# Layer-norm sums of a decoder step: chunks added elementwise on GpSimd before one product with ones on TensorE

## The reference

```python
def layer_norm(x, g, b):
    xf = x.astype(jnp.float32)
    mu = jnp.mean(xf, -1, keepdims=True)
    var = jnp.mean(jnp.square(xf - mu), -1, keepdims=True)
    y = (xf - mu) * lax.rsqrt(var + LN_EPS) * g.astype(jnp.float32) + b.astype(jnp.float32)
    return y.astype(x.dtype)
...
    def post_norm(x, delta, i, j):
        return layer_norm(ALPHA * x + delta, ln_gain[i, j], ln_bias[i, j])

    def half_ffn(x, i, f, j):
        return post_norm(x, 0.5 * swiglu(x, ffn_w_gate[i, f], ffn_w_up[i, f], ffn_w_down[i, f]), i, j)
...
        xp, xs = half_ffn(xp, i, 0, 0), half_ffn(xs, i, 0, 0)
...
        xp, xs = post_norm(xp, yp, i, 1), post_norm(xs, ys, i, 1)
        xp, xs = half_ffn(xp, i, 1, 2), half_ffn(xs, i, 1, 2)
```

## Time and profile before

| | |
|---|---|
| time, median of 3 runs | 3068.14 us (3064.81 to 3071.11) |
| the profiled execution | 3065.47 us, of which the span of instructions is 3063.6 us |
| PE busy | 2847.6 us, 93% of the span |
| DVE, ACT, POOL busy | 1034.4, 821.4 and 524.2 us (34%, 27%, 17%) |
| mean granted clock of PE | 0.964 |

### The profile page before, as it was taken

One profiled execution on the slowest core, in us unless ns is written; L12 is line 12 of the kernel. 1 busy time (PEld: TensorE's weight loads), 2 busy tenths in 40 slices (PEclk: granted clock), 3 DMA queues, 4 the chain that ended last, 5 costly groups with the idle time before them and its releaser, 6 DMA issues. The chain is left out here.

```text
span 3063.6 us, 56299 instructions
## 1 busy us (share of the span) xinstructions
PE 2847.6 (93%) x23010; PEld 2684.4 (88%) x23010; DVE 1034.4 (34%) x1683; ACT 821.4 (27%) x1590; POOL 524.2 (17%) x581
## 2 busy tenths in 40 slices
PE   8999999868999998999999999999967778899998
PEld 7999989748999998999989899989955447899998
DVE  2222233645222224222243424443442222522223
ACT  2222122623222212222122424242332221322222
POOL 3222102011222201222102021102110001222210
PEclk9999999979999999999999999999979888999999
DMA  7776624013666644666423142314247873466641
GB/s 248 241 246 182 222 67 98 4 50 108 221 220 209 200 133 153 210 219 223 156 67 91 44 125 78 95 40 120 83 149 277 293 275 109 154 220 207 229 143 42
DMA packets 460485, 478.73 MB, mean 156 GB/s; under 512 B 55886, under 2 KB 433951, under 8 KB 456120
## 3 DMA queue, kind: packets, MB, share of 16 engines
q1 hardware_dynamic: 454880, 464.85, 46.3%
q0 software_dynamic: 5392, 11.67, 1.3%
q10 hardware_dynamic: 64, 0.08, 0.0%
HBM read 463.55 MB, written 198.59 MB: 216 GB/s over the span
## 5 line engine op out<-in xcount | busy, mean ns | idle before, releaser
L703 PE MATMUL bank<-sb_xh,sb_wl 128*128 128x272 f32 x4416 | 957.7, 294 | 56.0 <-DVE sb_wl L1439 28.3
L707 PE MATMUL bank<-sb_xh,sb_wh 128*128 128x272 f32 x4416 | 943.5, 290 | 0.0
L705 PE MATMUL bank<-sb_xl,sb_wh 128*128 128x272 f32 x4416 | 941.7, 290 | 0.0
L1439 DVE TENSOR_TENSOR sb_wl<-sb_raw,sb_wh 128x1024 fp32r<-128x1024 f32 (+1 forms) x340 | 454.5, 1337 | 999.0 <-ACT sb_wh L1184 990.9
L703 PEld LDWEIGHTS bank<-sb_xh,sb_wl 128*128 128x128 f32 x4416 | 711.5, 191 | 64.4 <-DVE sb_wl L1439 31.7
L705 PEld LDWEIGHTS bank<-sb_xl,sb_wh 128*128 128x128 f32 x4416 | 712.6, 191 | 0.6
L707 PEld LDWEIGHTS bank<-sb_xh,sb_wh 128*128 128x128 f32 x4416 | 708.6, 191 | 0.0
L1184 ACT CAST sb_wh<-sb_raw 128x1024 fp32r<-128x1024 f32 (+1 forms) x340 | 376.6, 1110 | 980.4 <-PE bank L707 965.2
L703 PE MATMUL bank<-sb_hh,sb_wl 128*128 128x272 f32 x1408 | 312.9, 294 | 0.0
L705 PE MATMUL bank<-sb_hl,sb_wh 128*128 128x272 f32 x1408 | 304.9, 287 | 0.0
L707 PE MATMUL bank<-sb_hh,sb_wh 128*128 128x272 f32 x1408 | 304.7, 287 | 0.0
(11 more groups left out here) (240 smaller groups left out, 2273.3 us busy)
## 6 DMA issues: line engine op xcount, KB each, us to landing
out_state_b_s<-in_cache_b_kv SPq DMA_DIRECT2D x176, 704.0 KB, 6.3
sb_dkvb<-in_cache_b_kv SPq DMA_DIRECT2D x144, 512.0 KB, 6.3
sb_raw<-in_ffn_w_gate SPq DMA_DIRECT2D x88, 512.0 KB, 3.9
sb_raw<-in_ffn_w_up SPq DMA_DIRECT2D x88, 512.0 KB, 4.3
sb_raw<-in_ffn_w_down SPq DMA_DIRECT2D x64, 704.0 KB, 4.7
sb_raw<-in_attn_b_w_qkv SPq DMA_DIRECT2D x72, 512.0 KB, 3.9
out_state_b_s<-in_cache_b_kv SPq DMA_DIRECT2D x32, 1016.0 KB, 7.7
out_state_b_s<-in_cache_b_kv SPq DMA_DIRECT2D x44, 176.0 KB
```

Source lines behind the costliest of these rows:

```text
L703: pe.matmul(acc(s, h), wl[slot][:, k, :], hi(k)[:, halves[h]], start=start and k == 0, stop=False)
L705: pe.matmul(acc(s, h), wh[slot][:, k, :], lo(k)[:, halves[h]], start=False, stop=False)
L707: last = pe.matmul(acc(s, h), wh[slot][:, k, :], hi(k)[:, halves[h]], start=False, stop=end)
L1439: dve.tensor_tensor(wl[j % 2][:, 0:ph.chunks, :], raw[j][:, 0:ph.chunks, :], v.bitcast(F32), ALU.subtract).then_inc(wl_rdy, 1)
```

## The change

The chunks ahead of the last ones (seven of eight in a down phase, six of eight in a wo phase) no longer go through PE one by one. POOL adds them, chunk upon chunk, into `sil[0]`, and their squares into `sil[1]` (`sums` on POOL, behind `centre`), and PE takes one product of ones with each of the two (`sums` on PE, behind `half_done`, four matmuls). The last chunk or two go through `stats` by halves as before and add to the same banks. ACT's `square` now waits on POOL's additions (`q_add`) instead of PE's reads.

```diff
+            def sums(n):
+
+                pe.wait_ge(s_add, add0[n + 1])
+                for h in range(2):
+                    pe.matmul(bank[4 + h][:, 0:HALF], ones[:], sil[0][:, halves[h]], start=True, stop=False)
+                pe.wait_ge(q_add, add0[n + 1])
+                for h in range(2):
+                    mm = pe.matmul(bank[6 + h][:, 0:HALF], ones[:], sil[1][:, halves[h]], start=True, stop=False)
                 mm.then_inc(st_read, 1)
...
                     if i == 2:
                         centre(n)
-                    if i == 5:
-                        stats(n, 0)
-                    if i >= 5 and i % 2:
-                        stats(n, (i - 3) // 2)
                 weights_ready(14)
                 acc_ready(ph, n, 7)
                 part(14, (0,))
-                stats(n, 6)
                 weights_ready(15)
                 part(15, (0,)).then_inc(half_done, 1)
+                sums(n)
                 part(14, (1,), range(3))
-                stats(n, 7, (0,))
+                stats(n, 7, 0)
...
-                    if i >= 4:
-                        stats(n, 2 * i - 8)
-                        stats(n, 2 * i - 7)
                 for i in (6, 7):
                     pe.wait_ge(wl_rdy, ph.u0 + i + 5)
                     acc_ready(ph, n, i)
                     mm = part(i, (0,))
-                    if i == 6:
-                        stats(n, 4)
                 mm.then_inc(half_done, 1)
-                stats(n, 5)
+                sums(n)
                 part(6, (1,), range(3))
...
                 if m >= 2:
-                    act.wait_ge(st_read, sq_count(n, m - 2))
+                    act.wait_ge(q_add, add0[n] + max(m - 2, 1))
...
+            def sums(n):
+
+                pool.wait_ge(z0_rdy, n + 1)
+                for m in range(1, add0[n + 1] - add0[n] + 1):
+                    for h in range(2):
+                        pool.wait_ge(z_add[h], KC * n + m + 1)
+                    if m > 1:
+                        pool.wait_ge(s_add, add0[n] + m - 1)
+                    pool.tensor_tensor(sil[0][:], z[:, 0, :] if m == 1 else sil[0][:], z[:, m, :], ALU.add).then_inc(s_add, 1)
+                    pool.wait_ge(sq_rdy, sq_count(n, m))
+                    if m > 1:
+                        pool.wait_ge(q_add, add0[n] + m - 1)
+                    pool.tensor_tensor(sil[1][:], sqb[0][:] if m == 1 else sil[1][:], sqb[m % 2][:], ALU.add).then_inc(q_add, 1)
```

More of the change, by code:

```diff
@@ L234, in build @@
         c_mm, c_rdy, z_sh, z0_rdy = (sem(n) for n in ("c_mm", "c_rdy", "z_sh", "z0_rdy"))
-        sq_rdy, st_read = sem("sq_rdy"), sem("st_read")
+        sq_rdy, st_read, s_add, q_add = sem("sq_rdy"), sem("st_read"), sem("s_add"), sem("q_add")
         ln_msq, ln_dev, ln_rs, ln_nrm, ln_xh = (sem("ln_" + n) for n in ("msq", "dev", "rs", "nrm", "xh"))
@@ L456, in build @@
         TAIL = {"down": [(7, 0), (7, 1)], "wo": [(6, 0), (7, 0), (6, 1), (7, 1)]}
-        sq_events, sq0 = [], [0]
+        sq_events, sq0, st0, add0 = [], [0], [0], [0]
         for ph in phases:
@@ L462, in build @@
                 sq0.append(sq0[-1] + len(sq_events[-1]))
+                st0.append(st0[-1] + 1 + len(TAIL[ph.kind]))
+                add0.append(add0[-1] + first - 1)
         def sq_count(n, m, h=None):
@@ L466, in sq_count, with st_count @@
             return sq0[n] + (ev.index((m, None)) if (m, None) in ev else ev.index((m, h))) + 1
+        def st_count(n, m, h):
+            ev = sq_events[n]
+            return st0[n] + 2 + ev[add0[n + 1] - add0[n] + 1:].index((m, h))
         FIRST_KS = 3
@@ L568, in load_bias @@
                 if ps is pass_a or ps is pass_b[0]:
-                    sp.wait_ge(st_read, sq0[norm_index(0 if ps is pass_a else 1, 0) + 1])
+                    sp.wait_ge(st_read, st0[norm_index(0 if ps is pass_a else 1, 0) + 1])
                 else:
@@ L754, in centre, with stats @@
                 mm.then_inc(c_mm, 1)
[L756 to L766, removed]
-                mm.then_inc(st_read, 1)
+            def sums(n):
[5 more added lines that the diff above has]
+                    mm = pe.matmul(bank[6 + h][:, 0:HALF], ones[:], sil[1][:, halves[h]], start=True, stop=False)
+                mm.then_inc(st_read, 1)
+            def stats(n, m, h):
+                pe.wait_ge(z_add[h], KC * n + m + 1)
+                pe.matmul(bank[4 + h][:, 0:HALF], ones[:], z[:, m, halves[h]], start=False, stop=m == KC - 1)
+                pe.wait_ge(sq_rdy, sq_count(n, m, h))
+                pe.matmul(bank[6 + h][:, 0:HALF], ones[:], sqb[m % 2][:, halves[h]], start=False, stop=m == KC - 1).then_inc(st_read, 1)
             def acc_ready(ph, n, m):
@@ L807, in project_down @@
                     first_unit(ph.next, n + 1, range(FIRST_KS))
-                stats(n, 7, (1,))
+                stats(n, 7, 1)
             def project_wo(ph, n):
@@ L829, in project_wo @@
                     mm = part(i, (0,))
-                    if i == 6:
-                        stats(n, 4)
                 mm.then_inc(half_done, 1)
-                stats(n, 5)
+                sums(n)
                 part(6, (1,), range(3))
-                stats(n, 6, (0,))
-                stats(n, 7, (0,))
+                stats(n, 6, 0)
+                stats(n, 7, 0)
                 part(6, (1,), range(3, KC)).then_inc(mm_done, 1)
                 part(7, (1,)).then_inc(mm_done, 1)
-                stats(n, 6, (1,))
+                stats(n, 6, 1)
                 first_unit(ph.next, n + 1, range(FIRST_KS))
-                stats(n, 7, (1,))
+                stats(n, 7, 1)
             def tokens_major(R, b):
@@ L1206, in square @@
                 if m >= 2:
-                    act.wait_ge(st_read, sq_count(n, m - 2))
+                    act.wait_ge(q_add, add0[n] + max(m - 2, 1))
                 elif n:
-                    act.wait_ge(st_read, sq0[n])
+                    act.wait_ge(st_read, st0[n])
                 w = slice(0, TOK) if h is None else halves[h]
@@ L1213, in mean_square @@
             def mean_square(n, h):
-                act.wait_ge(st_read, sq_count(n, KC - 1, h))
+                act.wait_ge(st_read, st_count(n, KC - 1, h))
                 act.activation(sqb[0][:, halves[h]], bank[4 + h][:, 0:HALF], ACT.Square).then_inc(ln_msq, 1)
@@ L1928, in _ @@
                     centre(n_norm)
+                    sums(n_norm)
                     n_norm += 1
```

## The result

The changed kernel takes 3012.49 us (median of 4 runs, 3011.98 to 3014.24), the kernel before beside it 3067.77 (3064.81 to 3071.11): ratio 0.9819, 95% interval 0.9804 to 0.9835. That is 55.3 us faster where 61.8 were forecast. The time lies 7.5 us above the point and half a us inside the upper end of the forecast, 2996 to 3013; one of the four runs (3014.24) lies beyond it. The profiled execution took 3012.28 us, and its span is 3010.4 us.

The account below looks back on a forecast made before the run. PE was taken to bound the norm phases; 62.6 us of removed matmuls less 0.4 and 0.4 of waits gave 61.8 us, so 3003.7 or 3006.3, stated as 3005. The forecast range was 2996 to 3013 (0.83); 8 in 10, 2996 to 3020.

Parts of the forecast that it names:

- What is removed: PE's `stats` groups ahead of the half-0 tail: 11.04 us per down phase, 9.20 per wo phase, together 62.6 us.
- The small waits: PE waiting for unit 15's split, 0.1 us per down phase, and for POOL's last additions, 0.2 us per wo phase.
- POOL's additions in a down phase: The two additions for chunk 6, 1.74 us each with gap, end at about 420.7, hidden at no cost.
- the sign of being right: Among the signs listed for a right prediction: POOL's additions take 1.4 to 1.6 us.
- The cover of 4.6 us: End of a down phase: time left between POOL's last addition, about 420.7, and PE's product on `sil[1]`, 425.33.
- The first rival: POOL and DVE hold each other up in every addition, at 2.75 + 0.17 us each: 3025.9 us, chance 0.10.
- POOL in wo: End of a wo phase: POOL's last three additions end at 719.7 against PE's need at 719.51, cost 0.2 us.
- ACT's new wait: Squares wait for POOL's additions with ACT's weight splits queued behind: no cost, 4.2 us of cover at the tightest, in wo.
- the tail: Behind `half_done`, the chain from the last half-0 `stats` to POOL's scaling moves as a whole, keeping about 29 us.
- The slower rival: POOL sets the pace and the kernel is slower: 3083.7 us at 5.5 us per addition and gap, chance 0.03.
- The clock ... is no case of its own: Clock drops in the norm tails, 2.5 us each, may shift by norm; this only widens the forecast.
- The 6 us allowed for the tails: Clock drops in two or three of six norm tails, either way, as a widening of the forecast.

Follow-up runs that it names:

- dve_adds: The changed kernel with all 68 additions on DVE and none on POOL: 2999.83 us, ratio 0.9792 to the kernel before.
- pool_twice: The changed kernel with each of POOL's 68 additions made twice, first into an unused buffer: 3030.11 us, ratio 0.9890 to the kernel before.
- after_again: The changed kernel once more, unchanged, on another chip: 3000.95 us, ratio 0.9809 to the kernel before.

## Why the prediction was right, and where it was off

- **What is removed**, 11.04 us in a down and 9.20 in a wo phase: 10.97 and 9.16 measured (the first down phase 10.15, since its centring began 1.24 us later in the kernel before, and that stretch was 0.8 shorter there than in the other two). The six norms together gained 61.3 us where the sum said 61.8. This is shown, also by dve_adds.
- **The small waits**: 0.1 us was taken for unit 15 in a down phase, and some 0.08 is there, behind DVE's subtraction as the prediction had it; 11.04 less that is the 10.97 measured. For the 0.2 us of a wo phase there is nothing: PE has no idle time ahead of L767 and L770.
- **POOL's additions in a down phase**, 1.74 us with gap: there is no gap, and the additions of squares behind the first took 2.73 to 2.75 us, since DVE's split falls beside each of them. So the sign of being right that POOL's additions take 1.4 to 1.6 us did not come. The cover of 4.6 us hid it (4.0 left). The first rival had the mechanism right for every second addition, in a place where it costs 0.08 us.
- **POOL in wo**: 719.7 against 719.51 was said, it was 0.57 us early. By that margin another 0.2 us for each of the last three additions would begin to cost (an estimate; the nearest run is pool_twice, which is far over it).
- **ACT's new wait** and the tail: as said. ACT is idle ahead of a square only for DVE's additions to `z`, never for POOL, and the chain from the last half-0 product to the scaling kept its length (427.01 to 455.90, 28.9 us).
- **The slower rival**: not near. With two additions for one, the kernel is still 37 us faster than before.
- **The step that was mis-sized** is "The clock ... is no case of its own". It looked at the tails only, with 2.5 us for each. What moved was the first decode, a stretch the change doesn't touch: 6.8 us between the two profiles, and 8.1 and 7.6 between two profiles of one kernel, before and changed. Without it the forecast of 61.8 is met: 62.2 between before and after_again, 64.1 with the clock held.
- **Luck**: the sum and its mechanism are borne out phase by phase, but that the first time lies inside the forecast, by half a us, is partly luck. The 6 us allowed for the tails happen to be near the 6.8 that the decode took, for which the prediction had no row; after_again, at 3000.95, is on the other side of its point.

The Trainium skill (GPSIMD Engine Reference, 4.1 Engine selection) puts two-input elementwise work on VectorE, with GPSIMD about twice as slow. The prices agree (0.72 and 1.36 us), but dve_adds shows that the place changes nothing in a down phase and costs 0.8 us in a wo phase. The lock that the Trainium skill describes (SBUF — State Buffer, Who interferes with whom) is what the rows at 416.89 to 420.96 look like: each of the two engines waits until the other's instruction ends.

## What to carry to other kernels

Where one engine is busy throughout and another idle, an operation moved is worth its start-to-start cost on the first, as long as the second finishes before the first asks; work that out from the row of what is queued there, and the smallest cover decides (here the wo phase, 0.57 us). Look also at what the moved work slows beside it: DVE's split of unit 15 had no cover left, and PE waited 0.08 us for it. Compare stretch by stretch before a difference is put down to the change: a stretch that nothing touches can give back a tenth of the gain by its clock. And where the bounding engine stands idle behind a product, split the product by what the next chain needs first.

## What was not expected of the hardware

- The first decode ends with the clock at the level of 1.2 GHz or back at 2.4 GHz, in the same kernel, and a sequence takes 5.52 or 3.61 us by it. 36 and 14 idle matmuls ahead of it held the clock at 0.99 to 1.00 and saved 14 us of the changed kernel's stretch in the first profile (226.0 to 211.6), and 7 us of its stretch in after_again (218.4).
- After a wait of PE of 6.9 us in a wo tail of pool_twice, the next eight records took 0.70 us each in place of 0.39.
